# Reordering the first weight and modulation loads, and the chunk order of the first conv units, in a fused two-block kernel

## What is computed

```python
mod = silu(c) @ mod_w + mod_b                 # c (1,1024), mod_w (1024, 6*1024)
shift1, scale1, gate1, shift2, scale2, gate2 = split(mod, 6)
h = rms_norm(x, g_pre_mix) * (1 + scale1) + shift1
(sc_b, sc_c, sc_x, q, k, v, z, xbc, dt_raw, gl_a, gl_b, gl_c) = split_columns(h @ w_in)
# short convolution, stick-breaking attention and a Mamba-2 mixer on those columns,
# a gated merge, w_o, a residual, then a gated FFN with 22 hidden tiles of 128
```

## Time and profile before

| | before |
|---|---|
| median of 3 executions | 1259.59 us (1257.8 to 1261.81) |
| span of the profiled execution, first to last instruction | 1259.7 us |
| TensorE busy (matmuls) | 1119.6 us, 89% |
| VectorE busy | 856.8 us, 68% |
| ScalarE busy | 478.9 us, 38% |
| GpSimd busy | 470.5 us, 37% |
| moved by DMA | 413.08 MB, mean 328 GB/s |
| chain that ended last | TensorE 57%, DMA 27%, VectorE 9%, ScalarE 4% |

### The profile page before, as it was taken

One profiled execution on the slowest core, in us unless ns is written; L12 is line 12 of the kernel. 1 busy time (PEld: TensorE's weight loads), 2 busy tenths in 40 slices (PEclk: granted clock), 3 DMA queues, 4 the chain that ended last, 5 costly groups with the idle time before them and its releaser, 6 DMA issues.

```text
span 1259.7 us, 14772 instructions
## 1 busy us (share of the span) xinstructions
PE 1119.6 (89%) x4718; PEld 734.0 (58%) x4718; DVE 856.8 (68%) x1927; ACT 478.9 (38%) x1110; POOL 470.5 (37%) x355
## 2 busy tenths in 40 slices
PE   4999999989999997999899999887877878788776
PEld 3899899749999996864565555333322323233222
DVE  6584567546888878654987866848668577585454
ACT  2225242043333335532544444433433434334344
POOL 0144343023544552401354465444443535444410
PEclk8899999999999998999899999898998988989999
DMA  9666665564766873571999999999999999999994
GB/s 382 246 230 244 262 263 206 197 231 168 282 276 278 331 291 143 179 295 72 392 399 416 421 421 422 420 421 421 421 422 420 422 421 422 420 420 422 421 421 176
DMA packets 57230, 413.08 MB, mean 328 GB/s; under 512 B 6480, under 2 KB 6480, under 8 KB 7120
## 3 DMA queue, kind: packets, MB, share of 16 engines
q0 software_dynamic: 40608, 295.19, 57.0%
q1 hardware_dynamic: 16416, 116.88, 23.7%
q10 hardware_dynamic: 144, 0.26, 0.1%
HBM read 411.26 MB, written 1.05 MB: 327 GB/s over the span
## 4 chain that ended last, share of the span: by engine, by line
PE 57%; DMA 27%; DVE 9%; ACT 4%; issue 2%; SPq 0%; POOL 0%; DVEq 0%; ACTq 0%; POOLq 0%
PE ps L1057 15%; DMA areaB<-in_experts,idx 11%; PE ps L493 6%; PE ps L495 6%; DMA ring<-in_experts,idx 6%; PE ps L494 6%; DMA gate_area<-in_experts,idx 6%; PE ps L534 4%; PE ps L480 4%; DMA small<-in_experts,idx 3%; PE ps L752 2%; PE ps L598 2%; PE ps L968 2%; DMA areaB<-in_mod_w 2%; PE ps L460 1%
## 5 line engine op out<-in xcount | busy, mean ns | idle before, releaser
L1377 ACT ACTIVATE act<-now 128x1 f32<-128x1 f32 x256 | 50.9, 199 | 259.9 <-DVE now L2132 257.9
L1057 PE MATMUL ps<-areaB,mod_sum 128*128 128x512 f32 x248 | 122.3, 624 | 22.6 <-ACT mod_sum L1384 22.6
L1624 DVE SCALAR_TENSOR_TENSOR mod_sum<-mod_ring,cols,mod_sum 128x256 f32<-128x256 f32 x294 | 123.4, 495 | 0.0
L1465 POOL TENSOR_TENSOR w_lo<-ring,w_hi 128x512 fp32r<-128x512 f32 x41 | 99.8, 2449 | 61.4 <-ACT w_hi L1152 61.3
L1515 POOL DMA_INDIRECT areaB<-in_experts,idx x62 | 69.2, 1117 | 128.2 <-DVE idx L2069 61.5
L1057 PE MATMUL ps<-ring,mod_sum 128*128 128x512 f32 x204 | 100.3, 626 | 15.0 <-ACT mod_sum L1384 15.0
L1384 ACT ACTIVATE mod_sum<-small,act 128x128 f32<-128x128 f32 x256 | 102.8, 402 | 24.3 <-ACT act L1380 1.1
L1635 DVE TENSOR_TENSOR w_lo<-ring,w_hi 128x1536 fp32r<-128x1536 f32 x41 | 84.2, 2076 | 32.0 <-ACT w_hi L1152 32.0
L2132 DVE CUSTOM_DVE_ANT_0 areaB<-areaB,xn 128x1024 f32<-128x1024 f32 x62 | 75.5, 1224 | 43.1 <-DMA areaB<-in_experts,idx 42.8
L493 PE MATMUL ps<-hT_h,w_lo 128*128 128x256 f32 x352 | 99.4, 282 | 0.8 <-DVE hid_l L1865 0.8
L1057 PEld LDWEIGHTS ps<-areaB,mod_sum 128*128 128x128 f32 x248 | 45.5, 194 | 92.9 <-ACT mod_sum L1384 50.3
(11 more groups left out here) (390 smaller groups left out, 2480.0 us busy)
## 6 DMA issues: line engine op xcount, KB each, us to landing
ring<-in_stream SPq DMA_DIRECT2D x75, 1024.0 KB, 6.0
mod_ring<-in_mod_w POOLq DMA_DIRECT2D x24, 1024.0 KB, 6.7
mod_ring<-in_mod_w SPq DMA_DIRECT2D x18, 1024.0 KB, 6.0
gate_area<-in_mod_w SPq DMA_DIRECT2D x3, 1024.0 KB, 13.3
areaB<-in_mod_w SPq DMA_DIRECT2D x3, 1024.0 KB, 23.2
gate_area<-in_stream SPq DMA_DIRECT2D x3, 1024.0 KB, 13.0
mod_ring<-in_stream SPq DMA_DIRECT2D x2, 1024.0 KB, 11.4
small<-in_small SPq DMA_DIRECT2D x1, 1352.0 KB, 28.9
```

The source lines that it names most:

```text
L1057: last = mm(ps[:, B3 + 2 * t + b, :], spread_w[n // FEW % 2][:, n % FEW, :], row[ROW_OF[n]][:, D + 512 * b:D + 512 * b + 512], start=first ...
L1465: nc.gpsimd.tensor_tensor(w_lo[s][:, HALF:], slot[s][:, HALF:], w_hi[s][:, HALF:].bitcast(F32), ALU.subtract).then_inc(lo_pool, 1)
L1624: ins = V.scalar_tensor_tensor(out=o[n], in0=w, scalar=vec[:, k:k + 1], in1=o[n], op0=ALU.mult, op1=ALU.add)
```

## The change

Two edits. On the SP queue, pair 2 is issued ahead of conv unit 0, and pair 3 ahead of conv unit 1. In TensorE's list, the first part of conv unit 2 takes chunks 0 to 3 in place of 0 and 1, and its last part chunks 4 to 7 in place of 2 to 7. The number of transfers, of bytes and of matmuls stays as it was.

```diff
@@ -371,10 +371,10 @@
             sp.dma_start(x_sb, x).then_inc(x_in, 16)
             sp.dma_start(sm[:, n_c:n_late], small[:, n_c:n_late]).then_inc(small_in, 16)
             load_pair(1)
+            load_pair(2)
             first_load(0)
-            load_pair(2)
+            load_pair(3)
             first_load(1)
-            load_pair(3)
             first_load(2)
             sp.dma_start(sm[:, n_late:], small[:, n_late:]).then_inc(late_in, 16)
 
@@ -609,10 +609,10 @@
             xbc_part(1, 4, 5)
             mod_units(6, 7)
             pe.wait_ge(mod_read, 2)
-            xbc_part(2, 0, 1)
+            xbc_part(2, 0, 1, 2, 3)
             xbc_part(0, 6, 7)
             xbc_part(1, 6, 7)
-            xbc_part(2, 2, 3, 4, 5, 6, 7)
+            xbc_part(2, 4, 5, 6, 7)
             evacs[0] = 3
             proj_T("sc", 0)
             pe.wait_ge(evac, 3)
```

## The result

The changed kernel takes 1264.92 us (median of 10, 1262.77 to 1266.64) against 1259.95 us for the kernel before in the same series (median of 10, 1257.65 to 1262.35). The ratio is 1.0037, 95% interval 1.0026 to 1.0049: 3.3 to 6.2 us slower, 4.7 in the middle. It is real, and small. One of the 35 executions of the kernel before in a later series took 4802 us and is left out of every comparison.

A forecast was written before the change was run, and what follows sets the result against it. TensorE was taken to bound the front, gathers of expert rows the back, with front delays arriving whole at the end. Terms 0 + 3.9 + 0 + 0 = +3.9 us gave 1263.5 us, range 1258.5 to 1267.5.

The forecast's parts named there:

- Landings: Step 1, loads: conv unit 0 lands at 24.7, 5.0 us later; conv unit 1 goes back two places at no cost.
- The first part waits: Step 2, TensorE: first part waits until 24.75; after 4.6 us idle, half clock, 3.49 us, then sums 1.71.
- All behind moves along: Steps 3 and 4: columns of pair 1 at 30.05 in place of 26.14, all to the parts' end +3.9 us.
- The chunk order: Step 5: gain 0; conv unit 0 done 1.74 us later, delaying unit 3's load; taken as 0, bounds 0 and 0.9.
- the margin of 0.1 us: In step 5, time left between the landing of unit 3's load and TensorE wanting it.
- the base of the sum: The one profiled execution, span 1259.7 us, from whose times the +3.9 us was reckoned.
- If the clock returns as long after the sums as it did: Step 4's condition, behind the sums of pair 2: the 32 matmuls take 10.04 us again, and all is +3.9.
- step 4: From pair 2's products to the parts' end: everything 3.9 us later, the 32 matmuls again 10.04 us.
- A: Front, clock returns early: full from 31.29 gives -0.3 us, 1259.3; already at 24.75 gives -2.9, 1256.7; chance 0.2.
- C: Conv unit 0 lands no later than before, columns of pair 1 begin about 1.0 sooner: 1258.6; chance 0.05.
- B: From step 4, clock rises 3 us later, costing 1.5 more: 1265.5 to 1267.4; chance 0.15.

The follow-up runs named there:

- the loads alone: Only the load order of the change (pair 2 ahead of conv unit 0, pair 3 ahead of conv unit 1) on the kernel before: 1265.06 us, ratio 1.0044.
- pair 2 alone: Kernel before with only pair 2 moved ahead of conv unit 0, pair 3 left behind conv unit 1: 1264.53 us, ratio 1.0039.
- w_dt spread: Matmuls against w_dt spread among the last twelve calls of the unit ahead: on the kernel before 1257.79 us, 0.9978; on the changed kernel 1262.95 us, 1.0030.
- the denser kernel: Kernel before with pair 2 ahead of conv unit 0, six thrown-away matmuls, sums and parts reordered, matmuls against w_dt spread: 1257.78 us, ratio 0.9987.
- the chunk order alone: Only the chunk order of the change on the kernel before, loads as before: 1260.96 us, ratio 1.0004.
- one place: Kernel before with only modulation unit 4 ahead of conv unit 0, unit 5 behind it: 1261.68 us, ratio 1.0010.
- sums first: Changed kernel with the sums of pair 1 ahead of the first part in TensorE's list: 1259.91 us, ratio 1.0002.

## Why the prediction was right, and where its sum was short

The forecast was 1263.5, +3.9 us, slower by 0.31%; measured were +5.0 between the medians, or 0.37%. By its steps:

1. *Landings*: right. Conv unit 0 landed at 24.9 (24.7 foretold), the old place of unit 5, and conv unit 1 was late for nobody in the changed kernel.
2. *The first part waits*: right as a mechanism, idle 4.5 us (4.6 foretold), 3.60 us for the part (3.49 foretold). The sums behind it I took at half clock, 1.71, and they took 0.80. So the columns came at 29.45, not 30.05: +3.3 in the place of +3.9. The part, then, was at half clock as foretold, but the clock came up right behind it, which the sum did not have.
3. and 4. *All behind moves along*: right. The end of the 48 matmuls was 3.2 us later, and this distance stayed 3.0 to 3.5 us to the end. That the 32 matmuls took 9.91 us, the 10.04 of before, was luck: as the timelines have it they took 10.05 us here and 7.15, 9.01 and 8.84 in the three other profiles with this front (the loads alone, pair 2 alone, w_dt spread).
5. *The chunk order*: right, 0 by the run of it alone; the margin of 0.1 us was met to the tenth, and the denser kernel showed what lies beyond it, 1.4 us.

**What fell short** is the base of the sum. Its sentence "If the clock returns as long after the sums as it did" held in the profile of the changed kernel, as step 4 says by luck, but it made one profile stand for all. I took the half-clock stretch of one execution, 13.6 us, as that of the kernel. It was long for it. In three other kernels with nearly the old front it lasted 10.2 us (the chunk order alone), 3.4 us (one place) and 3.4 us (w_dt spread). The rows of the chunk order alone and of w_dt spread on the kernel before, fall and rise of each:

```profile
26.00:26.50 0.50, 0.00 (x0) 0.66 1.03 426
...
36.00:36.50 0.50, 0.50 (x3) 0.60 1.08 454
...
27.00:27.50 0.50, 0.23 (x1) 0.53 1.14 475
...
30.00:30.50 0.50, 0.50 (x3) 0.56 0.83 344
```

The front of before ended, by the start of the unit behind it, at 53.96 in the profile of before and at 52.69 and 50.14 in these two. The front with pair 2 moved ended at 57.33 (the changed kernel), 53.99 (the loads alone), 56.72 (pair 2 alone) and 55.58 (w_dt spread). So a pair of profiles can differ by anything from 0 to 7.2 us. The means, 52.3 and 55.9, are 3.6 apart, an estimate from three and four profiles that could be off by some 2 us: it fits the 3.9 of the sum and does not exclude the 5.0 of the medians. The profiled execution of before, 1259.7 + 1.7 = 1261.4 us by the same time around its span, was 1.4 us above the median of its ten; that of the changed kernel was 0.5 below its own. These 2 us are the difference between the 3.0 us of the two profiles and the 5.0 of the medians. That subtraction is all that is shown. Whether it was the long half clock of the front that put the profile of before above its median is open: no execution at the median was profiled. I also set the span beside the median as if they were one measure; 1.7 us lie between.

The rivals: A (the clock comes back early) came true in single executions, in the loads-only profile, and not in the median. C (the order of loads does not hold) fell with the landings. B (a late return) did not show in the profile. The size of the loss hangs on the clock, as feared: with the wait left in and the clock kept up over it by six useless matmuls, the ratio is 1.0003. The Trainium skill ("TensorE: Matmul & The Clock Gate", "What's actually happening") has activity release the slow clock; the runs agree in that adding matmuls in the waiting gap made the next part full speed (1.99 us in place of 3.60), and taking them from the dense list cost 2.6 us.

That +3.9 came as near to the measured +5.0 as it did owes something to luck. Of its two errors one made the loss too large (the sums at half clock, 0.6 us by the columns of pair 1) and one too small (the base, 1.4 us above the median of ten).

Three things are not settled: why the spread w_dt matmuls gain 2.8 us in the middle where the dip that they avoid explains about 1, why sums first gained nothing though its profile had the front done 2.8 us sooner, and whether one place of delay costs nothing or up to 3 us.

## What to carry to other kernels

In an engine's in-order list a transfer is due when its first reader stands in the list, and everything behind that reader is due with it: before a load is moved back, look at what stands behind its reader, here one column sum that the next five steps were waiting for. To get one input 5 us sooner by delaying another by 5 us gained nothing here, and where the list was changed with it only the loss went. And where an engine's clock depends on what it did before, the same wait can cost several times as much, here 1.3 us in a profile with the clock kept up (0.4 by the ratio, 2.0 at the most) and about 5 without; take several profiles before one of them is used as the base of a sum.

## What the runs showed of the hardware

- The granted clock of one and the same front differs from execution to execution: half for 13.6, 10.2 or 3.4 us with nearly the same work, and the front was over at 54.0, 52.7 and 50.1 us. How much of the scatter of 4 to 6 us in the kernel's times this makes is not shown.
- The eight matmuls right behind the transposes, 1.74 us at full clock and 3.49 at half, took 1.97, 2.11, 2.58, 2.74 and 2.80 us in five profiles with the same code up to there: the moment at which the clock comes up first differs from execution to execution.
- After 2.1 us of idleness, waiting for the ring, TensorE's next part ran at full clock (1.99 us in 2 of 2 profiles); after 4.5 to 4.6 us it ran at half (3.60 to 3.78 us in 4 of 4).
- Sixteen matmul calls of eight columns, 3.6 us long with TensorE 100% busy in the records, were followed by 3.4 us of half clock in 5 of 9 profiles (in one the clock fell 0.8 us before their end), which cost 1.7 us. Mixed with 256-column matmuls they were not, in 5 of 5.
- Ahead of the first change of clock that the records show, the clock view says 1.00, but the one-column sums at 15 us took 1.84 us, as those at half clock (1.71 to 1.87), and not the 0.95 to 1.05 of full clock. The duration is to be believed there.
